# When GpSimd makes the output weights' sums in two layers of a two-model kernel: a change of two waits

## The chip, the cores and the metric

The kernel runs on one core of one Trainium2 chip. The metric is device time in microseconds of one execution; smaller is better. Before the change it is 2863.14 us, the median of 3 runs (2861.01 to 2864.5).

## What is computed

Two transformer stacks run one behind the other on one sequence of 256 tokens of width 1024, all in float32. The first has four layers. Each projects `x`, attends within the sequence (12 heads) and to a memory of 256 rows (4 heads), projects the 1024 wide result with `w_out`, adds and normalises, and then runs a SwiGLU block. The kinds of attention rotate, so the first and the fourth layer are of the same kind, one in which each query keeps only its 64 best keys:

```python
score = jnp.einsum('bqhs,bqh->bqs', jax.nn.relu(dots), wi.astype(jnp.float32))
score = jnp.where(causal[None], score, -jnp.inf)
_, sel = lax.top_k(score, topk)
...
mixed = jnp.concatenate([mix.reshape(Bsz, S, MIX_WIDTH), mo.reshape(Bsz, S, MEM_WIDTH)], -1) @ w_out[i]
x = layer_norm(ALPHA * x + mixed, ln1_g[i], ln1_b[i])
```

The second stack (a recurrent mixer, latent attention, cross attention, mixtures of experts) isn't touched.

## The kernel before

Every engine has its own instruction list, written out in program order, and the lists meet only in semaphores. Nothing reorders them: an instruction that waits holds all that stands behind it on its engine. Weights come through `ring`, twelve slots of 128 x 2048 floats that SyncE's queue fills in order.

Many matrix products are made in seven products of quarters in place of eight. That needs sums of the weights' quarters and of the other factor's quarters. For the output projection GpSimd makes both, in `projection_sums`:

- `make_rows` runs once for each of the four slots that hold `w_out`: four subtractions of 128 x 512 (L2796 to L2799). The three sums of the first two slots go to `early_row_sums`, a part of `spare`. Those of the last two go to `late_row_sums`, where `xT` (the turned `x`) lies, and to a part of `proj`.
- `make_heads` runs four times behind that: four operations of 128 x 128 (L2804 to L2807), each time as soon as the attention has stored its blocks (`pair_stored`).

The input projection of the first and fourth layer is made in pieces by `chunk_by_seven`, and VectorE makes the weight sums that these need. The sums lie in turn in `spare` and in `arena` (`spare_sums`, `heads_sums`). TensorE's sixth product of a chunk is the last to read them, and it raises `chunk_middle`. The first layer's last chunk with sums in `spare` is its third; the fourth layer's is the second of three, ahead of which stands one more that was begun earlier.

In these two layers VectorE's list then holds, in this order: `rotate_tiles`, the rotary embedding of queries and keys (L2953 to L2959, twelve operations of 128 x 192, and behind them `rope_done`, for which TensorE waits before it turns the heads); `take_keys` for tile 0, pairs of L3101 and L3103 that find the best keys eight at a time; `add_chunk` of the last chunk (L3185); the last pair of `take_keys` and `mask_others(0)` (L3108 and L3110); seven pairs for tile 1; and then `attend_pairs`. That begins with the maxima of the two memory pairs (L3013), then the last pair for tile 1 with `mask_others(1)` (again L3108 and L3110), and then goes from pair to pair: copy of the turned exponents (L3028), masked maxima (L3018), inverse, store. In the fourth layer `rotate_tiles` stands behind the second chunk's `add_chunk`. In the first layer that order is the same, but the last of its twelve operations starts at 98.70 us, ahead of the third chunk's sixth product.

Of the semaphores, `pair_logits` is raised by TensorE once for each pair of heads whose logits are done, and `pair_maxima` by VectorE twice for each pair. `first` is the count of pairs before this layer.

Of the kernel before, what the change touches and what calls it, by code (L numbers as in the profile page):

```python
# [188 lines left out]
class Tally:  # L189
# [10 lines left out]
    def next(self, k=1):  # L200

        self.n += k
        return self.value()
# [32 lines left out]
def build(nc, A, out):  # L236
    ctx = ExitStack()
    with ctx:
# [72 lines left out]
        LATENT = 3  # L311
# [143 lines left out]
        sco = psum("sco", 2)  # L455
# [14 lines left out]
        pair_logits, pair_maxima, pair_exps = sem("pair_logits"), sem("pair_maxima"), sem("pair_exps")  # L470
        pair_turned, pair_PT_done = sem("pair_turned"), [sem("pair_first_PT_done"), sem("pair_second_PT_done")]
        pair_inverted, unit_inverted = sem("pair_inverted"), sem("unit_inverted")
        pair_summed, pair_stored = sem("pair_summed"), sem("pair_stored")
        unit_logits, unit_masked, unit_maxima = sem("unit_logits"), sem("unit_masked"), sem("unit_maxima")
        unit_exps, unit_added, unit_turned = sem("unit_exps"), sem("unit_added"), sem("unit_turned")
# [8 lines left out]
        chunk_summed, chunk_middle = sem("chunk_summed"), sem("chunk_middle")  # L484
# [101 lines left out]
        chunk_banks = []  # L586
# [285 lines left out]
        def _(pe):  # L872
# [58 lines left out]
                    if t == 0:  # L931
                        last.then_inc(pe_for_vec, 1)

            def output_products(kind, stored, behind_first, xT_free, loads=(1, 1, 1, 1), free_slots=0, bank_read=None):

                rows = []
                sums, heads = row_sums(kind), head_sums(kind)
                slots = []
                projection_slots.append((slots, stored, xT_free))

                def part(u, n):
                    (w11, third), (w21, w22) = quarters(rows[u])
                    h11, h12, h21, h22 = head_quarters(kind, u)
                    first, second, fourth = sums[u]
                    stationary = {1: h11, 2: h12, 3: heads[u][:, 2, :], 4: h22, 5: heads[u][:, 0, :], 6: heads[u][:, 1, :], 7: h21}[n]
                    moving = {1: w11[:, 0, :], 2: w21[:, 0, :], 3: w22[:, 0, :], 4: fourth, 5: first, 6: second, 7: third[:, 0, :]}[n]
                    return mm(out_banks[n], stationary, moving, start=u == 0, stop=u == 3)

                def await_sums():
                    pe.wait_ge(rows_made, t_rows_made.next())  # L950
                    pe.wait_ge(heads_made, t_heads_made.next())

                for u in range(4):
                    s = slot(loads[u])
                    slots.append((s, full[s].n))
                    rows.append(ring[:, s, :].rearrange("p (k n) -> p k n", k=2))
                    for produced in stored[u]:
                        pe.wait_ge(*produced)
                    if u == 0:
                        ins = part(u, 2)  # L960
                        if free_slots:
                            ins.then_inc(slots_used, free_slots)
                        await_sums()
                        part(u, 3)
                        behind_first()
                        part(u, 1)
                        part(u, 6)
                        if bank_read is not None:
                            pe.wait_ge(*bank_read)
                        part(u, 5)  # L970
                    elif u < 3:
                        part(u, 2)
                        part(u, 1)
                        await_sums()
                        for n in (3, 6, 5):
                            part(u, n)
                    else:
                        part(u, 1).then_inc(pe_for_act, 1)
                        part(u, 2)
                        await_sums()  # L980
                        part(u, 6).then_inc(pe_for_vec, 1)
                        part(u, 5).then_inc(pe_for_vec, 2)
                        part(u, 3).then_inc(pe_for_vec, 1)
                for u in range(4):
                    part(u, 7).then_inc(slots_used, 1)
                for u in range(4):
                    last = part(u, 4)
                last.then_inc(pe_for_vec, 1)
# [731 lines left out]
            def mla():  # L1720
# [58 lines left out]
                    pairs.append(([[(mlaT[r, b, :], mlaT[r, 8 + b, :]), (mlaT[r, 17 + b, :], mlaT[r, 16, :])] for r in both],  # L1779
                                  [[mla_v[:, k, 64 * (2 * b + e):64 * (2 * b + e) + 64] for k in range(NT)] for e in range(2)], True))  # L1780
                first, last_values = attend_pairs(pairs)
                output_products(LATENT, [[(pair_stored, first + 2 * u + 2)] for u in range(4)], last_values, (pair_logits, first + 1))

            def memory_attention(layer):
                def second_columns():
# [303 lines left out]
            for layer in range(FIRST_LAYERS):  # L2089
# [79 lines left out]
                if kind == 0:  # L2169
# [7 lines left out]
                    memory_left = memory_heads_inside()  # L2177
                    heads_left = sequence_heads()
                    homes = [heads_sums, spare_sums, heads_sums] if layer else [spare_sums, heads_sums, spare_sums]
                    chunk_by_seven(homes[0], xT, x_sums, False, layer == 0, {n: lambda: next(scores_left) for n in (2, 4, 7, 3)})  # L2180
                    chunk_by_seven(homes[1], xT, x_sums, False, False, {n: lambda: next(memory_left) for n in (2, 4)})
                    chunk_by_seven(homes[2], xT, x_sums, False, False, {n: lambda: next(heads_left) for n in (7, 5, 6)})
# [22 lines left out]
                if kind == 1:  # L2205
                    hold(1)
                    turn_unit(0)
                    pe.wait_ge(proj_done, t_proj.n + 2)
                    pe.wait_ge(unit_masked, len(UNIT_ITEMS))
                    first, last_values = attend_pairs(mem_pairs, behind_logits=lambda: unit_values(0, lin[:, 2:4, :], proj),  # L2210
                                                      banks_free=lambda: pe.wait_ge(unit_stored, 1), behind_turns=lambda: turn_unit(1))
                    last_values()
                    stored = [[(unit_stored, 1)], [(unit_stored, 1), (pair_stored, first + 1)],
                              [(pair_stored, first + 2), (unit_stored, 2)], [(unit_stored, 2)]]
                    output_products(kind, stored, lambda: unit_values(1, sco[:, :, :], proj), (unit_turned, 2), (2, 3, 3, 2), 1, (unit_stored, 2))
                else:
                    first, last_values = attend_pairs(mem_pairs + pairs, last_chunk)
                    output_products(kind, [[(pair_stored, first + 2 * u + 2)] for u in range(4)], last_values,
                                    (pair_logits, first + (1 if last_chunk is None else 2)))
                hold(2)  # L2220
                if layer + 1 < FIRST_LAYERS:
                    next_memory_kv(lambda: x_columns(0), lambda: x_columns(1, 2))
# [531 lines left out]
        def _(pool):  # L2754
# [52 lines left out]
                nc.gpsimd.tensor_tensor(fourth, h12, second, ALU.subtract).then_inc(heads_made, 1)  # L2807

            def projection_sums(kind):
                slots, stored, xT_free = projection_slots.pop(0)  # L2810
                for u, (s, loaded) in enumerate(slots):
                    pool.wait_ge(slot_full[s], loaded)
                    if u == (2 if kind else 0):
                        pool.wait_ge(*xT_free)
                    make_rows(ring[:, s, :].rearrange("p (k n) -> p k n", k=2), row_sums(kind)[u])
                for u in range(4):
                    for produced in stored[u]:
                        pool.wait_ge(*produced)
                    make_heads(head_quarters(kind, u), head_sums(kind)[u])
# [1174 lines left out]
```

## Time and profile before

| | before |
|---|---|
| median of 3 runs | 2863.14 us (2861.01 to 2864.5) |
| profiled execution, its own time | 2861.1 us |
| its span | 2859.0 us |
| TensorE busy | 2545.0 us (89%) |
| VectorE busy | 1274.0 us (45%) |
| ScalarE busy | 382.4 us (13%) |
| GpSimd busy | 211.7 us (7%) |
| TensorE on the chain that ended last | 72% |

The chain is the work followed back from the last instruction, at each step to what released it. An engine's busy share over the whole span says little about two stretches of some 50 us each, so the rows further down come from the timeline of those. Times there are from the span's start. Matmuls are pipelined and their ends are modelled. Spans on GpSimd are rough.

### The profile page before, as it was taken

How to read it: one execution, taken by the hardware profiler on the slowest of the kernel's cores; microseconds unless marked ns; L12 is line 12 of the kernel's file. 1: busy time of each engine (PE TensorE's matmuls, PEld its weight loads, DVE VectorE, ACT ScalarE, POOL GpSimd, SP SyncE). 2: the span in 40 equal slices, each digit the busy share in tenths (PEclk: the TensorE clock that was granted, in tenths of full speed). 3: DMA queues.
4: the chain of work that ended last, by engine and by line, in shares of the span. 5: the costliest groups of instructions: out<-in, count | busy, mean ns of one | idle time of the engine just before them, and what ended most of it. 6: DMA issues, size and time to landing. Idle time of an engine off the chain costs nothing.

```text
span 2859.0 us, 37977 instructions
## 1 busy us (share of the span) xinstructions
PE 2545.0 (89%) x16088; PEld 1646.6 (58%) x16088; DVE 1274.0 (45%) x2575; ACT 382.4 (13%) x847; POOL 211.7 (7%) x224
## 2 busy tenths in 40 slices
PE   9999999999999999999998999866667999766665
PEld 5769755796669947699457785322223675222221
DVE  4866644666466656877646633000002453000102
ACT  1410002100131001310022111000000412000000
POOL 0300012000120000400003000000000310000000
PEclk9999999999999999999999999978888999877888
DMA  8344543544535435264432658999999547999998
GB/s 318 119 157 159 186 138 124 187 159 156 191 101 180 177 121 198 93 192 160 160 109 98 236 226 313 421 421 421 421 421 389 190 183 272 421 421 421 421 421 341
DMA packets 245772, 703.57 MB, mean 246 GB/s; under 512 B 18795, under 2 KB 123753, under 8 KB 197219
## 3 DMA queue, kind: packets, MB, share of 16 engines
q1 hardware_dynamic: 244304, 699.30, 64.8%
q8 instruction: 129, 2.11, 0.3%
q10 hardware_dynamic: 1299, 1.83, 0.2%
q14 instruction: 40, 0.33, 0.0%
HBM read 698.20 MB, written 1.05 MB: 245 GB/s over the span
## 4 chain that ended last, share of the span: by engine, by line
PE 72%; DMA 21%; SPq 3%; DVE 2%; ACT 1%; issue 1%; DVEq 0%; ACTq 0%
PE lin L909 47%; PE sco L909 14%; PE trp L909 9%; DMA ring<-in_moe_w_up 6%; DMA ring<-in_moe_w_down 4%; DMA ring<-in_moe_w_gate 3%; DMA arena<-in_moe_w_down 3%; SPq L741 2%; DMA arena<-in_moe_w_gate 2%; PE trp L1078 1%; DMA arena<-in_moe_w_up 1%; DMA spare<-in_moe_w_gate 1%; PE trp L1174 1%; SPq L746 0%; SPq L743 0%
## 5 line engine op out<-in xcount | busy, mean ns | idle before, releaser
L909 PE MATMUL lin<-ring,arena 128*128 128x512 f32 (+4 forms) x2260 | 778.9, 542 | 17.6 <-DMA ring<-in_moe_w_down 8.8
L909 PEld LDWEIGHTS lin<-ring,arena 128*128 128x128 f32 (+1 forms) x2260 | 369.2, 177 | 346.5 <-issue 320.9
L909 PE MATMUL lin<-arena 128*128 128x128 f32 (+9 forms) x3312 | 459.5, 351 | 25.4 <-DMA ring<-in_moe_w_down 7.5
L909 PE MATMUL sco<-ring,arena 128*32 128x512 f32 (+2 forms) x1340 | 331.2, 784 | 158.5 <-DMA ring<-in_moe_w_up 53.4
L909 PE MATMUL sco<-arena 128*32 128x512 f32 (+6 forms) x1888 | 408.3, 466 | 54.8 <-DMA ring<-in_moe_w_gate 23.7
L909 PEld LDWEIGHTS lin<-arena 128*128 128x128 f32 (+4 forms) x3312 | 291.2, 164 | 104.0 <-issue 84.1
L3705 DVE TENSOR_TENSOR arena<-arena,sco 128x512 f32<-128x512 f32 x16 | 11.0, 688 | 759.1 <-PE sco L909 759.1
L909 PEld LDWEIGHTS sco<-ring,arena 128*32 128x32 f32 (+1 forms) x1340 | 89.2, 146 | 324.4 <-issue 322.1
L909 PEld LDWEIGHTS sco<-arena 128*32 128x32 f32 (+3 forms) x1888 | 160.0, 160 | 152.9 <-issue 145.3
L909 PE MATMUL trp<-arena 128*128 128x128 f32 (+2 forms) x1584 | 217.7, 292 | 1.1 <-ACT arena L2478 0.7
L2766 POOL TENSOR_TENSOR roots<-roots 128x1 f32<-128x1 f32 (+2 forms) x42 | 38.8, 925 | 2293.5 <-DVE roots L2888 2271.1
L909 PE MATMUL lin<-arena,ring 128*128 128x128 f32 (+1 forms) x1720 | 207.3, 284 | 0.0
L909 PEld LDWEIGHTS trp<-arena 128*128 128x128 f32 (+1 forms) x1584 | 175.6, 185 | 42.9 <-issue 41.4
L909 PEld LDWEIGHTS lin<-arena,ring 128*128 128x128 f32 (+1 forms) x1720 | 194.2, 188 | 8.4 <-issue 3.1
L909 PE MATMUL sco<-arena,ring 128*128 128x128 f32 x1152 | 136.7, 275 | 0.7 <-ACT arena L2293 0.7
L909 PEld LDWEIGHTS sco<-arena,ring 128*128 128x128 f32 x1152 | 132.8, 192 | 2.4 <-issue 1.4
L3124 DVE TENSOR_TENSOR arena<-ring 128x512 f32<-128x512 f32 x132 | 88.2, 695 | 71.2 <-PE sco L909 70.4
L909 PE MATMUL sco<-spare,arena 128*32 128x512 f32 (+2 forms) x192 | 95.2, 648 | 18.4 <-DMA ring<-in_moe_w_up 11.4
L2293 ACT ACTIVATE arena<-trp 128x512 f32<-128x512 f32 (+1 forms) x115 | 63.2, 590 | 353.8 <-PE trp L1078 353.7
L909 PE MATMUL lin<-spare,arena 128*128 128x256 f32 (+3 forms) x320 | 107.4, 486 | 2.4 <-DMA spare<-in_moe_w_down 2.4
L3128 DVE TENSOR_TENSOR ring<-ring 128x512 f32<-128x512 f32 x132 | 89.1, 703 | 1.5
L3130 DVE TENSOR_TENSOR arena<-ring,arena 128x512 f32<-128x512 f32 x132 | 88.1, 695 | 0.0
(365 smaller groups left out, 2395.6 us busy)
## 6 DMA issues: line engine op xcount, KB each, us to landing
ring<-in_w_gate_up SPq DMA_DIRECT2D x88, 1024.0 KB, 5.6
ring<-in_moe_w_up SPq DMA_DIRECT2D x82, 1024.0 KB, 26.7
ring<-in_moe_w_gate SPq DMA_DIRECT2D x75, 1024.0 KB, 27.0
arena<-in_moe_w_down SPq DMA_DIRECT2D x56, 1024.0 KB, 27.0
ring<-in_moe_w_down SPq DMA_DIRECT2D x51, 1024.0 KB, 26.7
ring<-in_w_down SPq DMA_DIRECT2D x44, 1024.0 KB, 5.2
arena<-in_moe_w_gate SPq DMA_DIRECT2D x44, 1024.0 KB, 26.7
arena<-in_moe_w_up SPq DMA_DIRECT2D x34, 1024.0 KB, 27.0
```

The costliest lines, as they stand in the source:

```text
L741: sp.dma_start(dst, src).then_inc(slot_full[s], 16)
L909: return nc.tensor.matmul(o, lhsT, rhs, start=start, stop=stop, skip_group_check=not one_group)
L1078: ins = nc.tensor.transpose(trp[0:src.free_size(), b, j * P:(j + 1) * P], src, ident[:, :])
L1174: last = nc.tensor.transpose(trp[:, e, to:to + P], pair_P[j % 3][:, e, lo:lo + P], ident[:, :])
L2293: nc.scalar.activation(dst, trp[0:rows, b, 0:n].rearrange("p (a b) -> p a b", a=shape[1]), ACT.Copy, scale=scale).then_inc(tr_done, 1)
L2766: nc.gpsimd.tensor_tensor(root_out[:, b, 0:n], root_in[:, b, 0:n], root_power[:, 0:n], ALU.pow).then_inc(root_done, 1)
L3124: V.tensor_tensor(first, w12, w11, ALU.subtract).then_inc(dve_step, 1)
L3128: V.tensor_tensor(w12, w22, w12, ALU.subtract)
L3130: ins = V.tensor_tensor(second, w22, first, ALU.subtract)
L3705: V.tensor_tensor(pair_h, pair_silu, sco[:, 1, :], ALU.mult).then_inc(h_done, 1)
```

## The change

In the first and fourth layer (`kind == 0`) GpSimd's one wait ahead of all four `make_rows` becomes two. The first two slots' rows now wait for `chunk_middle` at the count that says that the sums in `spare` have been read. The last two slots' rows wait for `pair_maxima` at `2 * first + 5`, which is the first half of the first causal pair (the third pair of the layer). The other layers' waits are written anew with the same meaning. No instruction is added or taken away.

```diff
@@ def output_products @@
-                projection_slots.append((slots, stored, xT_free))
+                projection_slots.append((slots, stored, rows_free))
@@ first stack, kind == 0 @@
+                    spare_read = len(chunk_banks) + (2 if layer else 3)
@@ first stack, kinds 0 and 2 @@
                     output_products(kind, [[(pair_stored, first + 2 * u + 2)] for u in range(4)], last_values,
-                                    (pair_logits, first + (1 if last_chunk is None else 2)))
+                                    {0: (chunk_middle, spare_read), 2: (pair_maxima, 2 * first + 5)} if kind == 0 else {2: (pair_logits, first + 2)})
@@ def projection_sums @@
-                slots, stored, xT_free = projection_slots.pop(0)
+                slots, stored, rows_free = projection_slots.pop(0)
                 for u, (s, loaded) in enumerate(slots):
                     pool.wait_ge(slot_full[s], loaded)
-                    if u == (2 if kind else 0):
-                        pool.wait_ge(*xT_free)
+                    if u in rows_free:
+                        pool.wait_ge(*rows_free[u])
                     make_rows(ring[:, s, :].rearrange("p (k n) -> p k n", k=2), row_sums(kind)[u])
```

The order of instructions is the same on every engine; what differs is what GpSimd waits for. In the first layer its list reads, before the change, from the first slot's rows on (`slot_full6` is the arrival of the weights in slot 6, `pool_step` GpSimd's own last operation):

```order
L2796 TENSOR_TENSOR spare<-ring 128x512 [waits pair_logits,slot_full6]
L2797 TENSOR_TENSOR ring<-ring 128x512 [waits pool_step]
L2798 TENSOR_TENSOR spare<-ring,spare 128x512
L2799 TENSOR_TENSOR spare<-ring,spare 128x512 [waits pool_step]
L2796 TENSOR_TENSOR spare<-ring 128x512 [waits slot_full7]
L2797 TENSOR_TENSOR ring<-ring 128x512 [waits pool_step]
L2798 TENSOR_TENSOR spare<-ring,spare 128x512
L2799 TENSOR_TENSOR spare<-ring,spare 128x512 [waits pool_step]
L2796 TENSOR_TENSOR arena<-ring 128x512 [waits slot_full8]
```

The same place after the change, whose file has one more line above it:

```order
L2797 TENSOR_TENSOR spare<-ring 128x512 [waits chunk_middle,slot_full6]
L2798 TENSOR_TENSOR ring<-ring 128x512 [waits pool_step]
L2799 TENSOR_TENSOR spare<-ring,spare 128x512
L2800 TENSOR_TENSOR spare<-ring,spare 128x512 [waits pool_step]
L2797 TENSOR_TENSOR spare<-ring 128x512 [waits slot_full7]
L2798 TENSOR_TENSOR ring<-ring 128x512 [waits pool_step]
L2799 TENSOR_TENSOR spare<-ring,spare 128x512
L2800 TENSOR_TENSOR spare<-ring,spare 128x512 [waits pool_step]
L2797 TENSOR_TENSOR arena<-ring 128x512 [waits pair_maxima,slot_full8]
```

Eight operations wait for the chunk, and the eight behind them for the maxima. In the fourth layer it is the same with slots 1 to 4 (`chunk_middle` with `slot_full1`, `pair_maxima` with `slot_full3`). There VectorE's list has, behind the `add_chunk` that waits for that same count of `chunk_middle`, the following, in the changed kernel's line numbers:

```order
L3186 TENSOR_TENSOR spare<-spare,lin 128x256 [waits chunk_middle]
L3186 TENSOR_TENSOR spare<-spare,lin 128x512 [waits proj_done]
L3186 TENSOR_TENSOR arena<-spare,lin 128x256 [waits dve_step]
L3186 TENSOR_TENSOR arena<-spare,lin 128x256
L3186 TENSOR_TENSOR arena<-spare,lin 128x256 [waits slots_used]
L2954 TENSOR_TENSOR arena<-arena,small 128x192 [waits proj_done]
L2955 TENSOR_TENSOR arena<-arena,small 128x192
L2956 TENSOR_TENSOR arena<-arena,small 128x192
L2957 TENSOR_TENSOR arena<-arena,small 128x192
L2959 TENSOR_TENSOR arena<-arena 128x24x8 [waits dve_step]
L2960 TENSOR_TENSOR arena<-arena 128x24x8
```

Nothing moved in this list; it shows what VectorE does once the semaphore has been raised for which GpSimd now waits too.

## Rows read from the trace of the kernel before

**Rows 1.** Chain that ended last, first layer: start us, us, what

```profile
121.63 1.46 DVE arena L3110
123.11 0.70 DVE arena L3028
```

**Rows 2.** Timeline of VectorE, first layer: start us, us, instructions, idle before

```profile
109.51 0.29 DVE L3108 TENSOR_SCALAR arena<-arena 128x256 f32<-128x256 f32 x1
109.84 0.43 DVE L3110 SCALAR_TENSOR_TENSOR arena<-arena,causal 128x256 f32<-128x256 f32 x1
...
117.57 1.29 DVE L3013 TENSOR_REDUCE small<-sco 128x2 f32<-128x512 f32 x2 [0.41 <-PE sco L909]
...
120.94 0.66 DVE L3108 TENSOR_SCALAR arena<-arena 128x256 f32<-128x256 f32 x1
```

**Rows 3.** Timeline of GpSimd, first layer, with the releaser of its wait

```profile
117.61 1.26 POOL L2796 TENSOR_TENSOR spare<-ring 128x512 f32<-128x512 f32 x1 [66.80 <-PE sco L909]
...
120.18 1.27 POOL L2798 TENSOR_TENSOR spare<-ring,spare 128x512 f32<-128x512 f32 x1
...
122.76 1.44 POOL L2796 TENSOR_TENSOR spare<-ring 128x512 f32<-128x512 f32 x1
...
137.20 1.27 POOL L2799 TENSOR_TENSOR arena<-ring,arena 128x512 f32<-128x512 f32 x1
```

**Rows 4.** Two lines of VectorE: ns min/median/max, first and last start us

```profile
L3101 DVE MAX8 small<-arena x32: 418/428/430, 99.0 to 1166.2; 128x8 f32<-128x256 f32 x32
...
L3018 DVE CUSTOM_DVE_ANT_0 arena<-sco,arena x24: 281/355/421, 123.7 to 1181.6; 128x128 f32<-128x128 f32 x12, 128x256 f32<-128x256 f32 x12
```

**Rows 5.** Timeline of the second layer, VectorE and one row of GpSimd

```profile
469.84 1.76 DVE L2985 TENSOR_TENSOR arena<-arena 128x512 f32<-128x512 f32 x1
471.63 1.38 DVE L2989 TENSOR_TENSOR arena<-arena 128x256 f32<-128x256 f32 x1
472.93 1.76 DVE L2989 TENSOR_TENSOR arena<-arena 128x512 f32<-128x512 f32 x1
...
471.13 1.60 POOL L2797 TENSOR_TENSOR ring<-ring 128x512 f32<-128x512 f32 x1
```

**Rows 6.** Timeline of TensorE, two rows of the first layer and two of the fourth

```profile
104.10 1.89 PE L909 MATMUL lin<-spare,arena 128*128 128x256 f32 x8
...
119.47 0.66 PE L1174 MATMUL trp<-ident,arena 128*128 128x128 f32 x4 [1.15 <-ACT arena L2317]
...
1135.67 3.62 PE L909 MATMUL lin<-spare,arena 128*128 128x256 f32 x16
...
1147.76 0.60 PE L1078 MATMUL trp<-ident,arena 128*128 128x128 f32 x4
```

**Rows 7.** Timeline of VectorE, fourth layer

```profile
1140.50 1.08 DVE L3185 TENSOR_TENSOR arena<-spare,lin 128x256 f32<-128x256 f32 x3
1141.62 0.36 DVE L2953 TENSOR_TENSOR arena<-arena,small 128x192 f32<-128x192 f32 x1
...
1144.95 0.35 DVE L2959 TENSOR_TENSOR arena<-arena 128x192 f32<-128x192 f32 x1
...
1153.61 1.27 DVE L3185 TENSOR_TENSOR arena<-spare,lin 128x256 f32<-128x256 f32 x3
...
1163.81 1.29 DVE L3013 TENSOR_REDUCE small<-sco 128x2 f32<-128x512 f32 x2 [0.40 <-DVE arena L3103]
...
1167.89 1.44 DVE L3110 SCALAR_TENSOR_TENSOR arena<-arena,causal 128x256 f32<-128x256 f32 x1
```

**Rows 8.** Timeline of ScalarE, fourth layer: end of the second memory pair's exponents

```profile
1168.64 0.25 ACT L2317 ACTIVATION_READ_ACCUMULATOR arena<-lin,small 128x1 f32 x1
```

**Rows 9.** Clock in the second layer: TensorE's timeline, then windows (busy by engine, PEclk)

```profile
476.40 0.66 PE L1174 MATMUL trp<-ident,arena 128*128 128x128 f32 x4 [2.00 <-ACT arena L2317]
...
478.00:480.00 2.00, 1.20 (x6) 1.09 (x7) 1.18 (x3) 1.64 (x8) 1.92 (x3) 0.50 0.00 0
482.00:484.00 2.00, 2.00 (x11) 1.04 (x8) 0.42 (x1) 0.00 (x0) 0.77 (x2) 0.50 0.00 0
```

More of the change, by code:

```diff
@@ L932, in output_linear, with output_products @@
                         last.then_inc(pe_for_vec, 1)
-            def output_products(kind, stored, behind_first, xT_free, loads=(1, 1, 1, 1), free_slots=0, bank_read=None):
+            def output_products(kind, stored, behind_first, rows_free, loads=(1, 1, 1, 1), free_slots=0, bank_read=None):
                 rows = []
@@ L1781, in mla @@
                 first, last_values = attend_pairs(pairs)
-                output_products(LATENT, [[(pair_stored, first + 2 * u + 2)] for u in range(4)], last_values, (pair_logits, first + 1))
+                output_products(LATENT, [[(pair_stored, first + 2 * u + 2)] for u in range(4)], last_values, {2: (pair_logits, first + 1)})
             def memory_attention(layer):
@@ L2214, in _ @@
                               [(pair_stored, first + 2), (unit_stored, 2)], [(unit_stored, 2)]]
-                    output_products(kind, stored, lambda: unit_values(1, sco[:, :, :], proj), (unit_turned, 2), (2, 3, 3, 2), 1, (unit_stored, 2))
+                    output_products(kind, stored, lambda: unit_values(1, sco[:, :, :], proj), {2: (unit_turned, 2)}, (2, 3, 3, 2), 1, (unit_stored, 2))
                 else:
```

## Prediction

> **What bounds the kernel now.** I read the page first: TensorE is busy 89% of the span and carries 72% of the chain, and GpSimd is busy 7%. So GpSimd's own work can't be the bound anywhere; what counts is what it does to others. I then followed the chain through the first layer and found one place where TensorE isn't its owner: behind the maxima of the memory pairs the chain runs through VectorE, over L3110 for 1.46 us and the copy L3028, for which TensorE's next turned block waits [rows 1]. The timelines of VectorE and GpSimd, laid side by side, say why. The same two operations, L3108 and L3110, take 0.29 and 0.43 us for tile 0, when GpSimd is idle, but 0.66 us and 1.46 us for tile 1 [rows 1, 2], when GpSimd makes its rows back to back from 117.61 on, some 1.27 us each [rows 3]. The GpSimd operation that starts at 120.18 ends at 121.45, and L3108 ends at 121.60. The next of GpSimd's is over when its successor starts, at 122.76, and L3110 ends at 123.09. So each of the two waits until an operation of GpSimd is through. GpSimd in turn takes 1.44 in place of 1.27 us once [rows 3]. The loss is 0.37 + 1.03 = 1.4 us, and it lies on the chain. The fourth layer has the same (L3110 1.44 us [rows 7]).
>
> Not every operation of VectorE is held. All 32 of L3101 take 418 to 430 ns and all 24 of L3018 in these layers 281 to 421 ns, with or without GpSimd's work beside them [rows 4]. L3101 reads one tensor of SBUF, and L3018 reads one there and one in PSUM. Held are L3110, which reads two tensors in SBUF, and L3108, which reads one but at a faster pace (0.29 us against 0.43 for as many columns).
>
> **What the change takes away.** The first eight operations of GpSimd run earlier, and the other eight start when the maxima behind L3110 are done. So L3108 and L3110 of tile 1 stand free in both layers: -1.4 us each. The work behind which the later eight then lie is L3028, L3018, L3039 and L3041, which read PSUM; by rows 4 that costs nothing. GpSimd ends its rows at about 134 in place of 138.47 us in the first layer [rows 3], so nobody comes to wait for them there; in the fourth the same distance from the maxima holds, and TensorE needs them only behind six pairs' attention. The rows are in the slots well before (GpSimd's wait for them ended on logits, not on a DMA), and SyncE's queue waits for no one new.
>
> **What it adds, first layer.** `chunk_middle` is raised when TensorE ends the sixth product at 104.10 + 1.89 = 105.99 [rows 6]. On the logits' event GpSimd starts 0.04 us behind VectorE (117.61 against 117.57 [rows 2, 3]), so I take 106.1, and it is busy until 116.4. VectorE reaches L3108 and L3110 of tile 0 there, at 109.51 [rows 2]. Two operations of GpSimd take 2.57 us (117.61 to 120.18), so its third ends at about 106.1 + 2.57 + 1.27 = 109.9 and its fourth 1.3 later, at 111.2. L3110 then ends 0.3 us behind it, at 111.5 or 111.6 in place of 110.27: +1.3 us. If GpSimd's grid lies otherwise, it is 0.9 to 2.1. What hides a part is VectorE's wait of 0.41 us ahead of the maxima [rows 2]. That leaves +0.9, and the 1.4 gained behind the maxima make it -0.5 us for the layer.
>
> **What it adds, fourth layer.** Here the semaphore comes a whole chunk earlier, at 1135.67 + 3.62 = 1139.29 [rows 6], and what VectorE does next is not `take_keys` but `rotate_tiles`: twelve operations, all of two SBUF tensors, from 1141.62 to 1145.30, 0.31 us each [rows 7]. GpSimd would run from 1139.4 on; its second operation ends at 1142.0, and six are left. The second layer shows what two such lists do to each other. VectorE's ends there are 471.60, 473.01 and 474.69 [rows 5]: one operation of GpSimd goes between any two of VectorE's. An operation of 256 columns comes to 1.41 us, one of 512 to 1.68. The difference is 0.27 for 256 columns, so a held turn costs 1.14 us and 192 columns 0.20: 1.34 us for each. The first rotation waits 0.3 us more than alone, and six turns follow: 6 x (1.34 - 0.31) = 6.2. So `rope_done` comes 6.5 us late, at 1151.8.
>
> Who waits? TensorE turns the first heads at 1147.76 [rows 6] and would stand until 1151.9: +4.1 us on it. VectorE is worse off: it goes on with `take_keys` 6.5 us late and gets back 0.2 at L3185, which before waited for TensorE (1.27 against 1.08 us [rows 7]), and 0.4 ahead of the maxima: they start 5.9 us late. TensorE's logits, which before came 0.4 us behind VectorE and are now 4.1 us late, are there by then. Less the 1.4 us behind the maxima, the copy L3028 is 4.5 us late. ScalarE's exponents, which end at 1168.89 [rows 8] and move by about 5.7, end with that copy and not behind it. The fourth layer loses 4.5 us.
>
> The bounds: no hold at all of the rotations would leave the gain, -1.2 us (ScalarE's 1168.89 is next, against the copy's end). If two short operations of VectorE slip into one gap, half of 6.2 goes and the layer ends at 3.1 + 0.3 - 2.0 = +1.4. If each turn costs a whole operation of GpSimd and the rotation on top (1.27 + 0.31), it is 6 x 1.27 + 0.3 = 7.9, less the 2.0 given back (0.2, 0.4 and 1.4): +5.9. I take the rows of the second layer, since they show the turns one by one with the same GpSimd operations.
>
> The Trainium skill (SBUF — State Buffer, section SBUF: two separate sides) says that VectorE, with two SBUF inputs or in its two-port mode, and GpSimd share a port pair as an exclusive lock held for the whole instruction. The rows above agree on who is held. By its whole instruction a turn would cost 1.27 and not 1.14 us, and the fourth layer about 0.8 us more, 5.3.
>
> **Sum.** -0.5 + 4.5 = +4.0 us. To it I add 0.5 for the clock, below. On the profiled execution's own 2861.1 us (span 2859.0, 2.1 around it) that is 2865.6. That execution was 2.0 us below the median of the runs, 2863.1, so the forecast for the median is 2867.6, or +0.16%. What this kernel's measurement tells from no change is about 0.2%, 5.7 us, which is 2857.4 to 2868.8.
>
> **The rivals.**
> *Forecast: GpSimd holds the rotations, and little comes on top.* 0.57; 2867.6, its own range 2865.0 to 2868.8.
> *The new standstill costs the clock too: slower by over 0.2%.* In the second layer TensorE waited 2.00 us, and the granted clock was 0.50, so 1.2 GHz, from 478 to 484 [rows 9]. The fourth layer gets a standstill of 4.1 us, and in the first the wait ahead of the first turned pair grows from 1.15 to 2.0 us (1.15 + 0.9). TensorE has 1.8 us in hand on VectorE in the fourth layer (5.9 - 4.1), so a fall right behind the standstill costs little; at the attention, where it is as slow as VectorE, 6 us at half clock would cost up to 3. It decides from 1.7 us on (5.7 - 4.0). Against it: the first layer's attention has a wait of 1.15 us [rows 6] at full clock, so not every wait does it. Halfway between nothing and 3 in one layer is what the forecast's 0.5 stands for, at a chance of one in three. With 3.4 from both layers on top of 4.0: 2870.5. Dearer turns, up to +5.9, lead to the same side. 0.28.
> *The rotations aren't held, or half.* Small operations may pass two at a time, or the 24 x 8 patterns be served otherwise; the trace never has a rotation beside GpSimd's rows. Then it is -0.5 - 1.2 = -1.7, or +0.9 with half: 2861.4 to 2864.0. For it speaks only that no row is the very case; against it the strict turns of rows 5. 0.12.
> *Faster by over 0.2%.* It would need 5.7 us, and all that GpSimd now costs on the chain here is 2.8. Only measurement gives it. 0.03.
>
> **How the numbers follow.** Faster by over 0.2%: 0.03. Slower: 0.28 and a share of the forecast's own upper edge, 0.32. Within 0.2%: 0.65. The range from 2863.0 to 2871.5 leaves out the case without any hold and the dearest falls of the clock.
>
> **What the changed profile would show.** GpSimd's first rows near 106 and 1139.4 and its ninth behind the first L3018. L3110 of tile 1 at 0.43 us in both layers, and that of tile 0 at about 1.4 in the first layer alone. Seven of the fourth layer's rotations at 1.3 us or so, with GpSimd's operations between them at up to 1.4, the last end near 1151.8, and TensorE idle 4 us for VectorE's L2960 (L2959 before). The pair loops at their pace of before. The prediction is wrong if the rotations keep 0.36 us, if VectorE reaches the fourth layer's maxima with less than 4 us delay, or if something behind the attention, a transfer or the clock, gives back or adds more than 1.5 us.

## The result

| | before | changed |
|---|---|---|
| median of 11 executions each, on one chip | 2861.47 us (2855.97 to 2867.04) | 2868.91 us (2863.51 to 2870.63) |
| profiled execution, its own time | 2861.1 us | 2866.83 us |
| its span | 2859.0 us | 2864.9 us |
| its mean granted clock | 0.946 | 0.938 |

The ratio is 1.0026, with a 95% interval of 1.0017 to 1.0034. The change makes the kernel slower, by about 7 us in this series. The ratio lies just beyond the 0.2% that I had named as the bound, and its interval reaches to both sides of that bound. Timed twice more, the same kernel came to 1.0015 [1.0004, 1.0025] and 1.0024 [1.0013, 1.0035]. Over all of its 35 executions the mean is 2867.5 us. Over 110 of the kernel before, from the same series, it is 2861.3 us. With standard deviations of 3.2 and 3.7 us that is +6.2 us, give or take 1.3 (95%).

The profiled execution changed comes to these places 1.7 to 2.3 us earlier than that of before. Its first product of weights starts 0.3 us earlier (9.21 against 9.49), and by 35.31 us, where that of before is at 37.62, it is 2.3 us ahead; all of this lies before anything that the change touches. So I compare two stretches and not clock times. **First stretch:** from the first mask operation of tile 0 (L3109, before L3108) to the attention's end, which is the first product of 128 x 512 of the output projection. **Fourth stretch:** from VectorE's pair of operations behind `chunk_middle` (L3186, before L3185) to the same product there. The rows of before that this needs beside [rows 2, 7] are these. Timeline of VectorE, kernel before:

```profile
1139.32 1.14 DVE L3185 TENSOR_TENSOR spare<-spare,lin 128x256 f32<-128x256 f32 x2 [2.70 <-PE lin L909]
```

Timeline of TensorE, kernel before, the first products of `w_out` in both layers:

```profile
142.70 1.55 PE L909 MATMUL lin<-ring,arena 128*128 128x512 f32 x3
...
1188.96 1.55 PE L909 MATMUL lin<-ring,arena 128*128 128x512 f32 x3
```

Before, the stretches are 142.70 - 109.51 = 33.19 us and 1188.96 - 1139.32 = 49.64 us.

### The profile page after: what moved, and what is told of

Read it like the earlier page. It is cut to its first block, busy times and chain, and to the rows that moved or that the text cites. A ratio compares the mean times of both kernels' runs of the same rounds, so it can differ in the third digit from the quotient of the medians.

```text
span 2864.9 us, 37979 instructions
## 1 busy us (share of the span) xinstructions
PE 2555.3 (89%) x16088; PEld 1651.0 (58%) x16088; DVE 1280.0 (45%) x2575; ACT 382.9 (13%) x847; POOL 212.0 (7%) x224
## 4 chain that ended last, share of the span: by engine, by line
PE 73%; DMA 19%; SPq 4%; DVE 2%; ACT 1%; issue 1%; DVEq 0%; ACTq 0%
PE lin L909 46%; PE sco L909 15%; PE trp L909 9%; DMA ring<-in_moe_w_up 6%; DMA arena<-in_moe_w_down 4%; DMA arena<-in_moe_w_gate 3%; DMA ring<-in_moe_w_gate 3%; SPq L741 3%; DMA ring<-in_moe_w_down 2%; PE trp L1078 1%; DMA arena<-in_moe_w_up 1%; PE trp L1174 1%; SPq L746 0%; ACT arena L2318 0%; ACT arena L2294 0%
## 5 line engine op out<-in xcount | busy, mean ns | idle before, releaser
L909 PE MATMUL sco<-ring,arena 128*32 128x512 f32 (+2 forms) x1340 | 338.5, 802 | 158.5 <-DMA ring<-in_moe_w_up 55.2
```

Of the source, the lines that this page charges most:

```text
L909: return nc.tensor.matmul(o, lhsT, rhs, start=start, stop=stop, skip_group_check=not one_group)
```

## The profile after

Timeline of VectorE in the changed kernel, first layer, then fourth:

```profile
107.21 0.63 DVE L3109 TENSOR_SCALAR arena<-arena 128x256 f32<-128x256 f32 x1
107.88 1.45 DVE L3111 SCALAR_TENSOR_TENSOR arena<-arena,causal 128x256 f32<-128x256 f32 x1
...
116.25 1.29 DVE L3014 TENSOR_REDUCE small<-sco 128x2 f32<-128x512 f32 x2
...
119.95 0.43 DVE L3111 SCALAR_TENSOR_TENSOR arena<-arena,causal 128x256 f32<-128x256 f32 x1
...
1137.60 1.14 DVE L3186 TENSOR_TENSOR spare<-spare,lin 128x256 f32<-128x256 f32 x2 [2.70 <-PE lin L909]
...
1139.90 0.67 DVE L2954 TENSOR_TENSOR arena<-arena,small 128x192 f32<-128x192 f32 x1
1140.49 1.42 DVE L2955 TENSOR_TENSOR arena<-arena,small 128x192 f32<-128x192 f32 x1
1141.83 1.42 DVE L2956 TENSOR_TENSOR arena<-arena,small 128x192 f32<-128x192 f32 x1
1143.17 1.42 DVE L2957 TENSOR_TENSOR arena<-arena,small 128x192 f32<-128x192 f32 x1
1144.62 1.31 DVE L2959 TENSOR_TENSOR arena<-arena 128x192 f32<-128x192 f32 x1
1145.86 1.41 DVE L2960 TENSOR_TENSOR arena<-arena 128x192 f32<-128x192 f32 x1
1147.30 1.31 DVE L2954 TENSOR_TENSOR arena<-arena,small 128x192 f32<-128x192 f32 x1
1148.54 0.35 DVE L2955 TENSOR_TENSOR arena<-arena,small 128x192 f32<-128x192 f32 x1
...
1149.73 0.35 DVE L2960 TENSOR_TENSOR arena<-arena 128x192 f32<-128x192 f32 x1
...
1168.91 1.29 DVE L3014 TENSOR_REDUCE small<-sco 128x2 f32<-128x512 f32 x2 [0.39 <-DVE arena L3104]
...
1172.62 0.43 DVE L3111 SCALAR_TENSOR_TENSOR arena<-arena,causal 128x256 f32<-128x256 f32 x1
```

Timeline of GpSimd in the changed kernel:

```profile
103.84 1.27 POOL L2797 TENSOR_TENSOR spare<-ring 128x512 f32<-128x512 f32 x1 [55.34 <-PE lin L909]
...
1137.71 1.28 POOL L2797 TENSOR_TENSOR spare<-ring 128x512 f32<-128x512 f32 x1 [34.03 <-PE lin L909]
...
1140.31 1.38 POOL L2799 TENSOR_TENSOR spare<-ring,spare 128x512 f32<-128x512 f32 x1
1141.77 1.26 POOL L2800 TENSOR_TENSOR spare<-ring,spare 128x512 f32<-128x512 f32 x1
1142.99 1.38 POOL L2797 TENSOR_TENSOR spare<-ring 128x512 f32<-128x512 f32 x1
1144.45 1.27 POOL L2798 TENSOR_TENSOR ring<-ring 128x512 f32<-128x512 f32 x1
1145.68 1.38 POOL L2799 TENSOR_TENSOR spare<-ring,spare 128x512 f32<-128x512 f32 x1
1147.13 1.26 POOL L2800 TENSOR_TENSOR spare<-ring,spare 128x512 f32<-128x512 f32 x1
```

Lay the two side by side between 1139 and 1149 us. The first rotation is held for 0.3 us (0.67 in place of 0.36). From the second, at 1140.49, to the eighth, at 1148.54, are six steps of 1.34 us on average, and in each step one operation of GpSimd stands between two rotations. The eighth starts behind GpSimd's last operation and takes 0.35 us again. So seven rotations are held, six of them for a whole turn. The twelve last from 1139.90 to 1150.08, 10.18 us, where they took 3.68 before [rows 7]. For tile 1 L3111 takes 0.43 us in both layers, where L3110 took 1.46 and 1.44 [rows 1, 7]. In the first layer tile 0 pays for that: 0.63 and 1.45 us against 0.29 and 0.43 [rows 2].

Timeline of TensorE in the changed kernel, first turned pair, first output product, then the fourth layer:

```profile
118.05 0.66 PE L1174 MATMUL trp<-ident,arena 128*128 128x128 f32 x4 [2.04 <-ACT arena L2318]
...
140.05 1.12 PE L909 MATMUL lin<-ring,arena 128*128 128x512 f32 x2
...
1144.31 1.89 PE L909 MATMUL lin<-ring,arena 128*128 128x256 f32 x8
1150.14 1.11 PE L1078 MATMUL trp<-ident,arena 128*128 128x128 f32 x4 [3.94 <-DVE arena L2960]
1151.04 3.62 PE L909 MATMUL lin<-arena 128*128 128x256 f32 x8
...
1192.83 1.98 PE L909 MATMUL lin<-ring,arena 128*128 128x512 f32 x4
```

TensorE stands for 3.94 us until the last rotation. Behind the standstill eight MATMUL records take 3.62 us that take 1.89 ahead of it. The windows of the same kernel say why; the third column from the end is the granted clock (PEclk, between POOL's busy time and the DMA share):

```profile
1148.00:1150.00 2.00, 0.00 (x0) 0.00 (x0) 1.97 (x6) 0.00 (x0) 0.40 (x1) 0.70 1.05 373
1150.00:1152.00 2.00, 1.86 (x7) 1.69 (x8) 1.86 (x8) 0.60 (x1) 0.00 (x0) 0.50 0.34 111
1152.00:1154.00 2.00, 2.00 (x6) 1.58 (x5) 1.86 (x7) 0.00 (x0) 0.00 (x0) 0.50 0.00 0
1154.00:1156.00 2.00, 2.00 (x9) 1.71 (x8) 1.86 (x7) 0.45 (x1) 0.00 (x0) 0.60 0.00 0
1156.00:1158.00 2.00, 2.00 (x13) 1.77 (x12) 1.80 (x6) 0.32 (x2) 0.00 (x0) 1.00 0.04 8
```

The clock is at 1.2 GHz for 6.8 us: the windows lack (0.30 + 0.50 + 0.50 + 0.40) x 2 = 3.4 us of full clock, and at half clock that takes twice as long. Windows of half a microsecond put the fall at about 1148.8, so it began 1.3 us before the standstill ended, and TensorE lost nothing in that part. From its first turned heads to its first logits TensorE took 17.54 us (1150.14 to 1167.68) where it took 14.81 before (1147.76 to 1162.57): the clock cost it 2.7 us.

The stretches of this execution are 140.05 - 107.21 = 32.84 us (-0.35) and 1192.83 - 1137.60 = 55.23 us (+5.59). Together +5.24 us. The span grew by 5.9, but that the two numbers are so near is partly chance: this execution is 1.72 us early at the fourth layer's chunk, and from the fourth layer's first output product to its end it takes 1672.1 us against 1670.0.

## The experiments

The kernels below were timed with 12 executions each (the change's first series with 11), against 11, 29 or 35 of the kernel before on the same chip. The table has, for each, its ratio, the two stretches of its profiled execution, and where in them the clock was at 1.2 GHz. "Attention" is behind TensorE's wait for ScalarE's first exponents, "turns" at the end of the standstill for the rotations and behind it.

| kernel | ratio [95%] | first, us | fourth, us | 1.2 GHz inside |
|---|---|---|---|---|
| before | | 33.19 | 49.64 | none |
| changed | 1.0026 [1.0017, 1.0034] | 32.84 | 55.23 | turns 6.8 us |
| changed, again | 1.0015 [1.0004, 1.0025] | 32.84 | 54.20 | turns 3.4 us |
| changed, third | 1.0024 [1.0013, 1.0035] | 33.88 | 55.17 | first attention 3.4, turns 6.8 us |
| first layer alone | 1.0005 [0.9992, 1.0019] | 33.99 | 49.63 | first attention 3.4 us |
| fourth layer alone | 1.002 [1.001, 1.003] | 33.20 | 54.23 | turns 3.4 us |
| behind the rotations | 1.0004 [0.9993, 1.0015] | 33.99 | 48.41 | first attention 3.4 us |
| one slot ahead | 1.0001 [0.9989, 1.0013] | 33.18 | 51.32 | fourth attention 3.4 us |
| eight idle products | 1.0012 [1.0, 1.0024] | 33.66 | 55.26 | first attention 3.4 us |
| four idle products | 1.0021 [1.0008, 1.0033] | 32.86 | 54.22 | none |
| all behind the maxima | 1.0029 [1.0019, 1.004] | 31.96 | 48.41 | none, but see below |
| between the masks | 0.9988 [0.9977, 0.9998] | 31.95 | 48.40 | none |
| between the masks, again | 0.999 [0.9979, 1.0001] | 31.96 | 48.40 | none |

**First layer alone and fourth layer alone.** Each has the new waits in one of the two layers, and the wait of before in the other.

```diff
-   {0: (chunk_middle, spare_read), 2: (pair_maxima, 2 * first + 5)} if kind == 0 else ...
+   ({0: (pair_logits, first + 1)} if layer else {0: (chunk_middle, spare_read), 2: (pair_maxima, 2 * first + 5)}) if kind == 0 else ...
```

The second has the two branches exchanged.

> The two waits are changed in the first layer alone; the fourth layer waits as before. If GpSimd's rows cost by holding VectorE's operations with two SBUF inputs (theory A), the first layer's stretch from L3109 of tile 0 to the first output product keeps the 32.84 us of the changed kernel (33.19 before), the fourth layer's from the chunk's L3186 to the first output product is the 49.64 of before, and the time is 0.4 us under before, which a measurement calls the same. If the loss of the changed kernel has its place in the first layer too or behind both (theory B: something later, such as the clock in the second stack, answers to any shift), this kernel is 1 us or more slower than before.

> The two waits are changed in the fourth layer alone. Theory A: the whole loss is here; the rotations take 1.3 us each seven times, the stretch from the chunk's L3186 to the first output product is 55.2 us against 49.64 before, and the time is some 5.6 us over before (ratio 1.0020), more than the changed kernel by 0.4. Theory B: less than half of the changed kernel's 7.4 us shows here.

The fourth layer carries the loss. Alone it costs 4.6 us in its stretch, the forecast's 4.5, and 0.2% in time (median 2865.58 against 2860.67 us). The 55.2 us that I expected for its stretch, the value of the change's own execution, didn't come: the clock fell for 3.4 and not for 6.8 us. The first layer alone didn't show the -0.5 us that I expected: its stretch was 0.8 us longer than before, since here the clock fell in the attention. Its ratio doesn't tell it from the kernel before in either direction. Theory B, a cost of 1 us or more that arises in the first layer or behind both, isn't excluded by it (median 2.0 us over before).

**Behind the rotations.** The fourth layer's first half waits for `rope_done`, so that no row of GpSimd meets a rotation; the first layer is as in the change.

```diff
-   {0: (chunk_middle, spare_read), 2: (pair_maxima, 2 * first + 5)}
+   {0: (rope_done, t_rope.n) if layer else (chunk_middle, spare_read), 2: (pair_maxima, 2 * first + 5)}
```

> As the changed kernel, but in the fourth layer GpSimd's first eight operations wait for rope_done, so that they run behind the rotations, beside take_keys. Theory A: the rotations take 0.36 us again, L3109 and L3111 of both tiles run alone, and the fourth layer's stretch becomes 48.4 us (49.64 less 1.2); the time is 1.2 + 0.4 = 1.6 us under before. If the loss came from the last eight operations' later start (theory C), the stretch stays above 50 us.

Timeline of GpSimd in this kernel, its first row in the fourth layer:

```profile
1145.70 1.27 POOL L2797 TENSOR_TENSOR spare<-ring 128x512 f32<-128x512 f32 x1 [40.05 <-DVE arena L2960]
```

The rotations take 3.69 us again and the stretch 48.41, 6.8 us less than in the change's own execution and 1.2 less than before. GpSimd runs its eight rows beside `take_keys`, and these cost VectorE nothing. So the place of the rows and not their number was what cost. Of the 1.6 us that I expected to gain, the first layer took 1.2 away again: its stretch was 33.99 us with a fall of the clock, where I had put 32.84.

**One slot ahead.** Fourth layer alone, with four operations of GpSimd ahead of the attention in place of eight.

```diff
+   ({0: (chunk_middle, spare_read), 1: (pair_maxima, 2 * first + 5)} if layer else {0: (pair_logits, first + 1)})
```

> Fourth layer alone: only the first slot's four operations are made behind the chunk, the other three slots' twelve behind the first causal maxima; the first layer waits as before. Theory A by its turns: when the rotations begin, two operations of GpSimd are left in place of six, so the rotations end 0.3 + 2 x 1.03 = 2.4 us late in place of 6.4, TensorE doesn't stand for them, the maxima start 1.8 us late, and the fourth layer's stretch is 49.64 + 1.8 - 1.4 = 50.0 us; the time is within 0.1% of before. If GpSimd's presence costs by a share of time and not by turns, the rotations end 3.2 us late (half). The heads' sums wait behind twelve operations now and end later; TensorE may wait for them at the first output product by up to 3 us, which would show as a wait there and not at the rotations.

Timeline of VectorE in this kernel:

```profile
1138.29 0.66 DVE L2954 TENSOR_TENSOR arena<-arena,small 128x192 f32<-128x192 f32 x1
1138.87 1.42 DVE L2955 TENSOR_TENSOR arena<-arena,small 128x192 f32<-128x192 f32 x1
1140.21 1.42 DVE L2956 TENSOR_TENSOR arena<-arena,small 128x192 f32<-128x192 f32 x1
1141.55 0.34 DVE L2957 TENSOR_TENSOR arena<-arena,small 128x192 f32<-128x192 f32 x1
```

Three rotations are held in place of seven, and the twelve take 6.12 us, 2.44 more than before: the price goes with the number of GpSimd's operations (0.3 us and two turns of 1.03, as expected; half would have been 3.2). The maxima start 26.38 us behind the chunk, 1.89 later than before. The stretch was still 1.3 us longer than expected. What TensorE's timeline and the windows show beside it is a longer wait ahead of the attention's first turned pair, and then half clock.

```profile
1164.17 0.66 PE L1174 MATMUL trp<-ident,arena 128*128 128x128 f32 x4 [1.74 <-ACT arena L2318]
```

```profile
1166.00:1168.00 2.00, 2.00 (x13) 1.35 (x10) 1.93 (x10) 1.52 (x6) 0.07 (x1) 0.51 0.00 0
1168.00:1170.00 2.00, 2.00 (x15) 1.34 (x13) 1.12 (x4) 2.00 (x9) 1.92 (x2) 0.63 0.00 0
```

**Eight, then four idle products.** The changed kernel, with products into a free bank ahead of the fourth layer's wait for the rotations, so that TensorE doesn't stand. They add work, and nobody reads their results.

```diff
+   if layer == 3:
+       await_transposes(1)
+       for _ in range(8):
+           mm(trp[:, tr_items[0] % 2, :], ident[:, :], causal[:, :, :].rearrange("p t k -> p (t k)"))
    pe.wait_ge(rope_done, ...)
```

> The changed kernel, and in the fourth layer TensorE makes eight products of 128 x 512 (0.43 us each, 3.4 together, of the identity and the mask, into a bank that the next turned block overwrites; no output depends on them) ahead of its wait for the rotations. If the fall of the clock behind the standstill is what put the changed kernel's stretch at 55.23 us, it is 54.2 us here: the rotations still end late (10.2 us of them), the clock stays at 1.00 in the windows behind them, and the maxima start 30.4 us behind the chunk's L3186 in place of 31.3. If the extra 1.0 us has another cause, 55.2 stays. The time is 1 us under the changed kernel's at most; within its noise.

> The changed kernel with four idle products of 128x512 on TensorE ahead of the fourth layer's wait for the rotations, in place of the eight tried before, which took 7.03 us and held TensorE until 3.4 us after the rotations. Four take 3.5 us, so they should end at the rotations' end (about 12.4 us behind the chunk) and leave less than 0.5 us of standstill. Theory (a fall of the clock behind the standstill is a cost of its own, up to 0.9 us when it lasts 6.8 us and none when it lasts 3.4 us, because VectorE's pairs set the maxima then): no stretch at 1.2 GHz between the chunk and the maxima, chunk to maxima 30.4 us, chunk to first output product 54.2 us, and a median 0 to 1 us below that of the changed kernel in the same call. Rival (the clock costs several us there, and is what the forecast left out): a median 2 us or more below the changed kernel's. Rival (the clock falls for another reason than the standstill): it falls in the stretch all the same, and chunk to output is up to 55.2 us.

Timeline of TensorE with eight:

```profile
1147.14 7.03 PE L909 MATMUL trp<-causal,ident 128*128 128x512 f32 x16
1154.01 0.60 PE L1078 MATMUL trp<-ident,arena 128*128 128x128 f32 x4
```

Timeline of TensorE with four, and under it VectorE's maxima in the same kernel:

```profile
1145.68 3.60 PE L909 MATMUL trp<-causal,ident 128*128 128x512 f32 x8
1149.77 0.66 PE L1078 MATMUL trp<-ident,arena 128*128 128x128 f32 x4 [0.49 <-DVE arena L2964]
```

```profile
1167.66 1.29 DVE L3018 TENSOR_REDUCE small<-sco 128x2 f32<-128x512 f32 x2
```

The first of the two missed its aim. The clock stayed up, but eight products were too many. One such product shows as two MATMUL records of 0.44 us, where I had counted one of 0.43, so they took 7.03 us and not 3.4. They ended 2.8 us behind the last rotation (1150.84 + 0.35 in VectorE's timeline of that kernel), and TensorE was as late as with the clock fallen. Its stretch of 55.26 us so said nothing on the clock. Four end just ahead of the rotations, the clock stays at 2.4 GHz, and the maxima start without a wait, 30.41 us behind the chunk. That is what the change has with 3.4 us at half clock too (30.40 in the second execution, 30.41 in the fourth layer alone); with 6.8 us it is 31.31 and 31.25. So up to the fourth layer's maxima a short fall costs nothing and a long one 0.9 us. In time four idle products stand 1.2 us below the changed kernel of the same series in the mean, with a standard error of 1.6, which shows only that the clock's fall there isn't worth several us.

**The changed kernel again and a third time.**

> The changed kernel once more, for a second profile and more times on the chip of the three others. Theory A with the clock: the first layer's stretch is 32.84 us where the clock stays up and 33.99 where it falls, the fourth's 54.2 to 55.3; the ratio to before lies at 1.0018 to 1.0026. If the 7.4 us of the first timing were all caused in these stretches, they would have to add up to more than the 5.2 seen in its profile.

> The changed kernel as it is, a third time, as the measure for the other two. Theory (the change costs what its two stretches show, 4.2 to 5.2 us, and the rest of the first difference of 7.4 us is scatter between executions): a ratio of 1.0014 to 1.0019 to the kernel before, fourth layer 54.2 to 55.2 us from the chunk to the first output product, first layer 32.8 to 33.7 us from the mask of tile 0 to that product. Rival (a cost outside of the two stretches of 2 us or more): a ratio of 1.0024 or more with the same stretches.

Timeline of TensorE in the third, first layer:

```profile
118.50 0.66 PE L1174 MATMUL trp<-ident,arena 128*128 128x128 f32 x4 [2.03 <-ACT arena L2318]
```

Its windows:

```profile
118.00:120.00 2.00, 1.25 (x7) 1.01 (x8) 1.97 (x5) 2.00 (x9) 0.00 (x0) 0.82 0.51 175
120.00:122.00 2.00, 2.00 (x11) 1.06 (x9) 1.45 (x4) 1.67 (x7) 0.00 (x0) 0.50 0.00 0
```

The wait of 2.03 us is the same as in the first execution (2.04 at 118.05), and here the clock falls behind it and there not. The third execution's ratio of 1.0024 is the rival's number with the theory's stretches at their long end, so it decides for neither. The second execution's stretches add up to 4.2 us, and its series was 6.6 us over before by the medians: the two stretches don't carry all of that difference.

**All behind the maxima.** All sixteen rows wait for the first causal maxima, in both layers.

```diff
-   {0: (chunk_middle, spare_read), 2: (pair_maxima, 2 * first + 5)}
+   {0: (pair_maxima, 2 * first + 5)}
```

> Both layers: all sixteen operations of GpSimd wait for the first causal maxima, none is made ahead of the attention. L3109 and L3111 run alone for both tiles and the rotations too, so the stretches up to the first output product are 32.0 and 48.4 us. But the rows then end some 20.6 us behind the maxima, and the first heads' sums 2 us later, at about the 145 us where TensorE wants them at 141.5: I expect a wait of TensorE for GpSimd of about 3 us in each layer, behind the first output product, and a time 2 x (3 - 1.2) = 3.6 us over before. If no such wait is there, the split into halves wasn't needed and the time is 2.4 us under before.

Timeline of TensorE in this kernel, the output projection's second step in both layers:

```profile
144.87 2.05 PE L909 MATMUL lin<-ring,arena 128*128 128x512 f32 x2 [3.27 <-POOL arena L2808]
...
1192.45 2.04 PE L909 MATMUL lin<-ring,arena 128*128 128x512 f32 x2 [3.24 <-POOL arena L2808]
```

Both stretches are as short as any in the table, and the ratio is its highest (1.0029). The gain comes back behind the stretch as a wait for GpSimd's heads, 3.3 us in each layer where I expected 3, and in either layer the clock is at 1.2 GHz for 3.4 us from just before its end. That makes the loss larger than the 3.6 us expected: the medians differ by 9.1 us. The waits less the gains are 2 x (3.3 - 1.2) = 4.2 us, and if TensorE sets the pace there, two falls add at most 3.4, an estimate. So half of the rows does have to run ahead of the maxima.

**Between the masks.** The first half waits for a new semaphore that `mask_others(0)` raises, in both layers, so that it runs beside tile 1's `take_keys` alone. The second half is as in the change.

```diff
-   {0: (chunk_middle, spare_read), 2: (pair_maxima, 2 * first + 5)}
+   {0: (tile_masked, 3 if layer else 1), 2: (pair_maxima, 2 * first + 5)}
```

Not shown: the new semaphore's declaration, and that the last operation of `mask_others` raises it, in place of VectorE's own counter, and waits for it.

> Both layers: the first eight operations wait for the end of mask_others(0) (a new semaphore on its last operation), the other eight for the first causal maxima. GpSimd's eight take 10.3 us and between the two masks lie 10.7 us of VectorE (L3102, L3104 and L3014), none of which was held in any trace. Theory A: L3109 and L3111 of both tiles at 0.29 and 0.43 us, rotations at 0.36, stretches 32.0 and 48.4 us, so 2.4 us (0.08%) under before, too little for the timing to tell; TensorE's wait ahead of the first turned pair stays at 1.15 us, so the clock doesn't fall in the first layer's attention as it did in two of the kernels with the changed first layer. If GpSimd's work beside the maxima cost something that L3014's rows don't show, the stretches are longer.

> The version in which the first half's rows wait in both layers until tile 0's mask is stored, a second time. If its gain is that of the two stretches (1.2 us in the first layer, 1.2 us in the fourth): stretches of 32.0 and 48.4 us, and a ratio of 0.9990 to 0.9993 to the kernel before, so 6 to 8 us below the changed kernel. If the first measurement was luck: a ratio of 0.9998 or more, with one of the stretches near that of the kernel before (33.2 or 49.6 us).

Timeline of VectorE in its first execution, both masks of the first layer:

```profile
107.48 0.30 DVE L3111 TENSOR_SCALAR arena<-arena 128x256 f32<-128x256 f32 x1
107.81 0.43 DVE L3113 SCALAR_TENSOR_TENSOR arena<-arena,causal 128x256 f32<-128x256 f32 x1
...
118.90 0.29 DVE L3111 TENSOR_SCALAR arena<-arena 128x256 f32<-128x256 f32 x1
119.23 0.42 DVE L3113 SCALAR_TENSOR_TENSOR arena<-arena,causal 128x256 f32<-128x256 f32 x1
```

GpSimd's eight rows lie between the masks, from 108.38 to 118.72. No operation of VectorE is held, TensorE's wait ahead of the attention stays at 1.15 us, and both stretches are 1.2 us below those of before: 2.4 us in all. Measured were 2856.39 us against 2861.64 and 2858.57 against 2860.74, 9 to 12 us below the changed kernel. Both ratios agree with the 2.4 us (0.9992); that it beats the kernel before is shown once by its interval and not quite the second time. Its two profiled executions have the same stretches, and spans of 2850.7 and 2859.8 us. Of those 9.1 us 7.7 arise behind the fourth layer's first output product (1666.5 against 1674.1 us from there to the end), in instructions that are the same in both. That is the scatter against which any change here is measured. Part of it may be the clock: within each of the three long series of the kernel before, slower executions have a lower mean granted clock (correlations of -0.37, -0.63 and -0.66). No run separates that.

## Why the prediction was right, and where not

**Mechanism and direction: right.** GpSimd's rows held the rotations by strict turns. The last rotation ended at 1150.08 us. The chunk's operations came 1.72 us earlier than before (1137.60 against 1139.32), so on the time scale of before that is 1151.80, the 1151.8 forecast. The first rotation was held for 0.3 us and six more for a turn of 1.34 us each, as forecast. TensorE stood 3.94 us for 4.1. The maxima were 5.9 us late (30.40 - 24.49) in the execution with the short fall, as forecast, and the 1.4 given back behind them measured 1.2 to 1.4. Fourth layer alone: +4.59 us for +4.5. The Trainium skill (SBUF — State Buffer, section SBUF: two separate sides) says that the port pair is held for the whole instruction; by that the layer would have lost 5.3 us, an estimate. The trace doesn't agree on the duration: a turn took 1.34 us, for a pair of operations that take 1.27 and 0.31 alone. The rival of unheld rotations is refuted.

**First layer: right by its terms.** From the mask of tile 0 to the maxima it was 9.04 us for 8.06, +0.98 (forecast +0.9), and behind them 23.80 for 25.13, -1.33 (forecast -1.4). At full clock that is -0.35 for -0.5. GpSimd started within 0.04 us of VectorE's operation on the same semaphore, and L3111 took 1.45 us, as worked out.

**The clock: mis-sized.** The term that was off is "To it I add 0.5 for the clock". At half clock for 3.4 us TensorE loses up to 1.7 us, and that fits into the 1.8 that it had in hand in the fourth layer: up to the maxima it cost nothing, where I had written little. But the fall lasted 6.8 us in two of three executions. TensorE lost 2.7 of it, 0.9 more than it had in hand, the 0.39 us wait ahead of the maxima came back, and the layer paid 1.0 us. In the first layer the longer wait that I had forecast, 2.0 us, came (2.04), and behind it the clock fell in four of the seven profiled kernels that have it. Three of the seven are executions of the change, and it fell in one of them. Where it fell, the first stretch was 0.8 to 1.15 us longer (33.66 to 33.99 against 32.84 to 32.86). Behind the wait of 1.15 us, which the six others have, it never fell. Over the three executions of the change the clock's part is 1.03, 0 and 2.01 us, 1.0 in the mean. The forecast gave it half of that. The rival gave it 3.4 us, more than any of the three shows. Its mechanism is real, its price was too high. Why the same wait is followed by a fall in one execution and not in the next stays open.

**The sum.** -0.35 and +4.56 (54.20 - 49.64) and 1.0 for the clock make 5.2 us, where the forecast had 4.5. The timing says 6.2, give or take 1.3. The missing 1 us is within that; whether it has a place outside the stretches wasn't settled. From the fourth layer's first output product to the end the three profiles of the change take 1672.1, 1677.3 and 1675.0 us, against 1670.0 in the one profile of before. That is over the 1.5 us that the prediction named as a sign of being wrong. But that part of the program scatters by as much without the change (1666.5 and 1674.1 us between the masks), so the sign can't be judged, and a cost there is neither shown nor excluded.

The forecast of 2867.6 us lies 1.3 us below the measured 2868.91, and the range from 2863.0 to 2871.5 holds it. That it is so near is in part luck. It stood on the kernel before at 2863.14 us, the median of three runs; eleven runs beside the change gave 2861.47. As differences, 4.5 us was forecast, and 7.4 measured in this series or 6.2 over all three. And I called "within 0.2%" the likeliest, and the ratio says 1.0026: the case with 0.32 came in, by a margin smaller than the interval. A forecast of +0.16% so close to the bound, with a term for the clock that could only add, should have had the two cases nearer to even.

## What to carry to other kernels

Before an idle GpSimd is given work early, look at what VectorE does from the semaphore on. Here each of GpSimd's 1.27 us rows cost VectorE about 1 us beside operations with two SBUF tensors, and nothing beside the key searches and reads of PSUM. The place is worth more than the engine's idle time. And a standstill of 2 to 4 us on TensorE is to be priced twice: once for itself, and once for a stretch at 1.2 GHz that may follow, less what TensorE has in hand on the engine that ends last. Such a stretch cost 0 to 1.15 us in the change's layers.

## What the runs showed of the hardware

- **Turns are per operation, not per time.** Eight rows of GpSimd held seven rotations of 192 columns, four rows held three; the first of them was held for 0.3 us only, each other for 1.03. A held pair took 1.34 us, 0.24 less than the 1.27 + 0.31 of the two alone.
- **GpSimd pays too, but little.** Its rows of 1.27 us took 1.38 in every second place beside the rotations, and 1.45 once beside L3111.
- **The same wait does not always bring the same clock.** A wait of 2.03 to 2.06 us in the same place of the program was followed by 3.4 us at 1.2 GHz in four of seven profiled executions. Where the wait was 1.15 us it never fell there (six executions). With the standstill of 3.9 us came 3.4 us at that level in two executions and 6.8 in two; the long ones began 1.3 to 1.5 us before the standstill ended. With four or eight idle products in the standstill's place the clock didn't fall there.
